# Two-layer hybrid block: the sums of squares in the gated delta rule as two fp32r matmuls of high and low parts

## What is computed

```
def l2_normalize(x):
    return xf * lax.rsqrt(jnp.sum(xf * xf, axis=-1, keepdims=True) + EPS)
...
qkv = jax.nn.silu(causal_short_conv(g_qkv, conv_w))
gq, gk, gv = split(qkv)                    # 8 heads of 128 each
gq = l2_normalize(gq) * 128 ** -0.5
gk = l2_normalize(gk)
o_gdn = gated_delta_rule_chunked(gq, gk, gv, g, beta)
o_gdn = rms_norm_2(o_gdn, gdn_norm_g) * silu(z)
```

## Time and profile before

| | |
|---|---|
| median of 3 runs | 1613.04 us |
| lowest and highest | 1610.92 and 1615.45 us |
| the profiled execution | 1611.96 us, its span 1609.8 us |
| mean granted TensorE clock of the span | 0.997 |
| delta rule in the span | from about 836 to 1239 us |

### The profile page before, as it was taken

One profiled execution on the slowest core, in us unless ns is written; L12 is line 12 of the kernel. 1 busy time (PEld: TensorE's weight loads), 2 busy tenths in 40 slices (PEclk: granted clock), 3 DMA queues, 4 the chain that ended last, 5 costly groups with the idle time before them and its releaser, 6 DMA issues.

```text
span 1609.8 us, 23976 instructions
## 1 busy us (share of the span) xinstructions
PE 1572.8 (98%) x9289; PEld 1258.7 (78%) x9289; DVE 1146.2 (71%) x1742; ACT 762.7 (47%) x1179; POOL 231.8 (14%) x206
## 2 busy tenths in 40 slices
PE   8999999999999999999999999999999999999999
PEld 5778778888888877667677878878787888888887
DVE  5867764867676787887767677585775477777768
ACT  6444444736363656325555345353443373626263
POOL 0544320000000002233200504005050000000000
PEclk9999999999999999999999999999999999999999
DMA  5222225323232412223113132131220351414131
GB/s 156 77 66 67 67 65 174 114 93 116 90 120 71 126 46 66 66 66 94 27 49 93 27 83 67 55 91 52 68 67 27 119 168 54 145 65 144 66 105 53
DMA packets 196816, 135.39 MB, mean 84 GB/s; under 512 B 9627, under 2 KB 184236, under 8 KB 196708
## 3 DMA queue, kind: packets, MB, share of 16 engines
q1 hardware_dynamic: 196708, 133.90, 27.8%
HBM read 131.70 MB, written 2.18 MB: 83 GB/s over the span
## 4 chain that ended last, share of the span: by engine, by line
PE 79%; DVE 11%; ACT 4%; issue 3%; DMA 1%; POOL 1%; SPq 0%; POOLq 0%; ACTq 0%; DVEq 0%; PEldq 0%
PE bank L244 10%; PE bank L246 10%; PE bank L245 10%; PE bank L1187 6%; PE bank L1189 6%; PE bank L1188 6%; PE bank L351 4%; PE bank L353 4%; PE bank L352 4%; PE bank L2193 4%; DVE arena L2500 3%; DVE w_lo L228 2%; ACT w_hi L224 2%; PE bank L2019 1%; PE bank L1748 1%
## 5 line engine op out<-in xcount | busy, mean ns | idle before, releaser
L228 DVE TENSOR_TENSOR w_lo<-raw,w_hi 128x1024 fp32r<-128x1024 f32 x152 | 191.5, 1260 | 73.0 <-ACT w_hi L224 71.8
L244 PE MATMUL bank<-m_hi,w_hi 128*128 128x512 f32 x584 | 231.8, 397 | 8.8 <-DVE w_lo L228 4.4
L245 PE MATMUL bank<-m_lo,w_hi 128*128 128x512 f32 x584 | 228.2, 391 | 0.0
L246 PE MATMUL bank<-m_hi,w_lo 128*128 128x512 f32 x584 | 228.2, 391 | 0.0
L224 ACT CAST w_hi<-raw 128x1024 fp32r<-128x1024 f32 x168 | 175.2, 1043 | 85.7 <-PE bank L246 48.9
L1219 ACT CAST d_hi<-arena 128x1024 fp32r<-128x1024 f32 x112 | 117.7, 1051 | 130.1 <-PE bank L1189 130.1
L1224 DVE TENSOR_TENSOR d_lo<-arena,d_hi 128x1024 fp32r<-128x1024 f32 x112 | 135.8, 1217 | 10.1 <-ACT d_hi L1219 10.0
L244 PEld LDWEIGHTS bank<-m_hi,w_hi 128*128 128x128 f32 x584 | 110.1, 188 | 38.5 <-DVE w_lo L228 10.8
L244 PE MATMUL bank<-h_hi,w_hi 128*128 128x512 f32 x344 | 135.4, 394 | 1.0 <-DVE w_lo L228 1.0
L246 PE MATMUL bank<-h_hi,w_lo 128*128 128x512 f32 x344 | 134.0, 390 | 0.0
L245 PE MATMUL bank<-h_lo,w_hi 128*128 128x512 f32 x344 | 134.0, 389 | 0.0
(11 more groups left out here) (352 smaller groups left out, 3333.2 us busy)
## 6 DMA issues: line engine op xcount, KB each, us to landing
raw<-in_w_in SPq DMA_DIRECT2D x64, 512.0 KB, 3.8
raw<-in_l_w_ff SPq DMA_DIRECT2D x32, 512.0 KB, 4.1
arena<-in_l_w_ff SPq DMA_DIRECT2D x32, 512.0 KB, 5.6
raw<-in_w_mlp_up SPq DMA_DIRECT2D x32, 512.0 KB, 4.0
arena<-in_w_mlp_down SPq DMA_DIRECT2D x32, 512.0 KB, 5.5
raw<-in_l_w_in SPq DMA_DIRECT2D x24, 512.0 KB, 3.8
raw<-in_l_w_out SPq DMA_DIRECT2D x8, 512.0 KB, 4.1
arena<-gb_rows SPq DMA_DIRECT2D x16, 256.0 KB, 4.7
```

The costliest lines, as they stand in the source:

```text
L228: dve.tensor_tensor(w_lo[q.par][:], raw[q.par][:], w_hi[q.par][:].bitcast(F32), ALU.subtract).then_inc(s["w_ready"], 1)
L244: pe.matmul(g_bank[q.par][:], w_hi[q.par][:, k], hi[:, k], start=(k == 0), stop=False)
L245: pe.matmul(g_bank[q.par][:], w_hi[q.par][:, k], lo[:, k], start=False, stop=False)
L246: last = pe.matmul(g_bank[q.par][:], w_lo[q.par][:, k], hi[:, k], start=False, stop=(k == KT - 1))
```

## The change

Both kinds of sums are made as two fp32r matmuls: the tile of squares is split into a high part (rounded by ScalarE) and a low part (subtracted by VectorE), each is multiplied by a matrix of ones in fp32r, and the two accumulate in one bank. For the keys the cast stands on ScalarE right behind the square, and the subtraction on VectorE at u = 2 and u = 4, between `silu` and `dve_split`. For the outputs the casts stand on ScalarE between `out_squares` and `out_roots`, and the subtractions on VectorE between `out_total` and `out_gate`; TensorE makes the sums after k = 5 instead of k = 3 of panel 0 (for the last pair the place stays). The new tiles lie in memory that is not in use at that time (`l_hi2` over `rr`, `l_lo2` in place of the key squares, `t_hi2` over `kb`, `t_lo2` in place of the output squares). So that the places fit, `ub` grows from 516 to 544 elements, which moves what follows it in the arena by 28 elements.

```diff
+        ones_r = sb("ones_r", [P, P], F32R)
...
-        ub = take(SEQ + CONV)
+        ub = take(SEQ + 32)
...
             def l2_sum(p, e):
-                pe.wait_ge(s["l_sq"], 2 * p + e + 1)
-                pe.matmul(b[2 * e][:], ones[:], sq2[:, e], start=True, stop=True).then_inc(s["l_ss"], 1)
+                pe.wait_ge(s["l_lo"], 2 * p + e + 1)
+                pe.matmul(b[2 * e][:], ones_r[:], l_hi2[:, e], start=True, stop=False)
+                pe.matmul(b[2 * e][:], ones_r[:], l_lo2[:, e], start=False, stop=True).then_inc(s["l_ss"], 1)
...
             def out_sums(p):
                 for e in range(2):
-                    pe.wait_ge(s["oo_t"], 2 * p + e + 1)
-                    pe.matmul(b[2 * e][:], ones[:], o_sq[:, e], start=True, stop=True).then_inc(s["oo_ss"], 1)
+                    pe.wait_ge(s["oo_tl"], 2 * p + e + 1)
+                    pe.matmul(b[2 * e][:], ones_r[:], t_hi2[:, e], start=True, stop=False)
+                    pe.matmul(b[2 * e][:], ones_r[:], t_lo2[:, e], start=False, stop=True).then_inc(s["oo_ss"], 1)
...
-                            if k == 3 and u == 0:
+                            if k == 5 and u == 0:
                                 out_sums(p - 1)
...
                 act.activation(sq2[:, e], qkv[:, 3 * e + 1], ACT.Square).then_inc(s["l_sq"], 1)
+                act.wait_ge(s["l_sq"], 2 * p + e + 1)
+                act.copy(l_hi2[:, e], sq2[:, e]).then_inc(s["l_hi"], 1)
...
+            def out_sum_high(p):
+                for e in range(2):
+                    act.wait_ge(s["oo_t"], 2 * p + e + 1)
+                    act.copy(t_hi2[:, e], o_sq[:, e]).then_inc(s["oo_th"], 1)
...
                     out_squares(p - 1)
+                    out_sum_high(p - 1)
                     out_roots(p - 1)
...
+            dve.tensor_copy(ones_r[:], ones[:]).then_inc(s["memsets"], 1)
             dve.sem_inc(s["ub0"], 1)
...
+            def out_sum_low(p, e):
+                dve.wait_ge(s["oo_th"], 2 * p + e + 1)
+                dve.tensor_tensor(t_lo2[:, e], o_sq[:, e], t_hi2[:, e].bitcast(F32), ALU.subtract).then_inc(s["oo_tl"], 1)
+
+            def l2_low(p, e):
+                dve.wait_ge(s["l_hi"], 2 * p + e + 1)
+                dve.tensor_tensor(l_lo2[:, e], sq2[:, e], l_hi2[:, e].bitcast(F32), ALU.subtract).then_inc(s["l_lo"], 1)
...
                     out_total(p - 1, 0)
                     out_total(p - 1, 1)
+                    out_sum_low(p - 1, 0)
+                    out_sum_low(p - 1, 1)
                     out_gate(p - 1)
...
                     if u:
                         silu(p, u - 1)
+                    if u in (2, 4):
+                        l2_low(p, u // 2 - 1)
                     dve_split(dve, gdn_panel(p, u + 2))
                     conv(p, u)
```

More of the change, by code:

```diff
@@ L149, in build @@
                 nc.sbuf_tensor("d_lo1", [P, 2, SEQ], F32R) as d_lo1:
+            pass
+        with nc.sbuf_tensor("sum_room0", [P, 2048], F32), nc.sbuf_tensor("l_hi2", [P, 2, SEQ], F32R) as l_hi2, \
+                nc.sbuf_tensor("l_lo2", [P, 2, SEQ], F32R) as l_lo2, nc.sbuf_tensor("sum_room1", [P, 7200], F32), \
+                nc.sbuf_tensor("t_hi2", [P, 2, SEQ], F32R) as t_hi2, nc.sbuf_tensor("t_lo2", [P, 2, SEQ], F32R) as t_lo2:
             pass
@@ L2131, in build @@
         gc_b, be_b = take(2, SEQ), take(2, SEQ)
+        assert at[0] == 2048
         rr, sq2 = take(2, SEQ), take(2, SEQ)
@@ L2138, in build @@
         dec = [take(TT, P) for _ in range(2)]
+        assert at[0] == 11296
         kb, ek = take(2, SEQ), take(2, SEQ)
@@ L2165, in build @@
              "dm_b dm_c dec_r ek_a ek_b ek_c kk_ps kk_r qk_ps qk_r kbe_r qd_r tok_ps tok_sb al_r yy_ps y_sb2 "
-             "z_ps t_r u_ps2 u_sb w_sb ws_ps vn_r kv_ps st2 oo_ps oo_sq oo_q oo_t oo_ss oo_ln oo_r oo_y2 oo_y3 oo_y4 oo_hi "
+             "z_ps t_r u_ps2 u_sb w_sb ws_ps vn_r kv_ps st2 oo_ps oo_sq oo_q oo_t oo_th oo_tl l_hi l_lo oo_ss oo_ln oo_r oo_y2 oo_y3 oo_y4 oo_hi "
              "gdn_done", reuse=True)
@@ L2477, in act_gdn @@
             out_squares(PAIRS - 1)
+            out_sum_high(PAIRS - 1)
             out_roots(PAIRS - 1)
@@ L2486, in dve_gdn @@
                 dve.memset(t_f[e][bot, :, 0:CHUNK], 0.0).then_inc(s["memsets"], 1)
-            dve.wait_ge(s["memsets"], 7)
+            dve.wait_ge(s["memsets"], 8)
             def conv(p, u):
@@ L2687, in dve_gdn @@
             out_total(p, 1)
+            out_sum_low(p, 0)
+            out_sum_low(p, 1)
             out_gate(p)
```

## The result

| | before | changed |
|---|---|---|
| median of 8 runs | 1612.93 us | 1617.82 us |
| lowest and highest | 1609.56 and 1615.45 | 1615.36 and 1620.37 |
| ratio of the runs | | 1.0033, 95% interval 1.0020 to 1.0046 |
| profiled execution, and its span | 1611.96, 1609.8 | 1619.75, 1617.9 |

The kernel became slower by 4.9 us by the medians and 5.3 by the ratio (0.0033 x 1613), with an interval of 3.2 to 7.4. It lies at the bound of what can be told from no change (0.3%, 4.8 us).

The account below looks back on a forecast made before the run. The ScalarE and VectorE loop was taken to set the pace up to panel 7, not PE. Loop and tail (+3.8 us) plus two clock falls (+2.9) gave +6.7 on 1613.04: 1619.7 us, range 1614.8 to 1623.8.

Parts of the forecast that it names:

- my own forecast: The loop's loss plus one to four clock falls: 1618.3 to 1622.6 us, given chance 0.52.
- rival 1: Panel 5 of each pair: stalls stay without a clock fall, only the loop counts; 1616.8 us, chance 0.30.
- The bound: Up to panel 7 in every pair, the ScalarE and VectorE loop sets the pace, though PE is 98% busy.
- rival 2: PE is the bound after all, decided at panel 7; its 6.5 us saving counts: 1606.5 us, chance 0.04.
- u = 4: VectorE's new subtraction ahead of panel 6's split delays the loop 0.61 us in each of four pairs: 2.4 us.
- The loop's start: Output sums two eighths later delay logarithms and `conv_in(0)`: 0.68 us in each of three pairs, 2.0 us.
- The stall: PE waits about 2.5 us mid panel 5 for head 1's low part, each pair; hidden with 0.13 to spare.
- Rival 3: Panel 5's stall is not hidden: 0.5 us more per pair; 1621.7 with two falls, 1624.6 with four; chance 0.12.
- rival 4: Ones in fp32r cost 0.86 per matmul, like fp32; PE works 6.5 us more: about 1626, chance 0.02.
- The tail: Last pair's output sums: PE and the roots come earlier despite a 0.13 wait, -0.65 us.
- Sum without the clock: Loop at u = 4, loop's start and tail: 4 x 0.61 + 3 x 0.68 - 0.65 = +3.8 us.
- The clock: After panel 5's stalls: two of four followed by a fall of PE's clock, 1.45 us each, +2.9 us.

Follow-up runs that it names:

- both half changes: The change for the key sums alone (1614.68 us against 1612.73) and for the output sums alone (1613.61 us), each with the other sums as before.
- keys only: Against the kernel before: key sums split as in the change, output sums left as one fp32 matmul each after k = 3; 1614.68 us against 1612.73, ratio 1.0016.
- the kernel without the stall, sum behind panel 6: The change with the key sum of head 1 moved on PE from the middle of panel 5 to behind panel 6; 1618.90 us, ratio 1.0041.
- the loop in a better order: VectorE's convolution ahead of the split: 1604.34 us with fp32 sums, 1602.04 with only output sums split; a mixed order with both sums split, 1596.84.
- outputs only: Against the kernel before: output sums split as in the change, after k = 5, key sums left as before; 1613.61 us, ratio 1.0002.
- low part at u = 5: The change with head 1's key sum behind panel 6 and its subtraction on VectorE moved from u = 4 to u = 5; 1613.48 us, ratio 1.0005.
- output sums after k = 3: The change with the output sums moved back from k = 5 to k = 3 of panel 0; 1614.47 us against 1613.44, ratio 1.0013.
- all three places: The change with head 1's low part at u = 5, its sum behind panel 6, and output sums after k = 3; 1611.15 us, ratio 0.9989.

## Why the prediction was right, and where its sizes were off

The measured 1617.8 lies in the range, but under the span that I gave my own forecast (one to four falls, 1618.3 to 1622.6) and nearer to rival 1 (1616.8).

- **The bound.** Right. Against 98% busy, the loop of ScalarE and VectorE sets the pace up to panel 8; rival 2 (PE is the bound) is out by both half changes. One reading was wrong: of the "4.9 us in 6 waits" for `w_lo` only four, 2.8 us, stood before panel 7; one stood in pair 0 (1.16) and one behind the last pair (0.97).
- **u = 4.** Forecast 0.61 a pair, measured 0.60.
- **The loop's start.** Forecast 0.68, measured 0.68. Cast, subtraction and sums took the times of the rows; PE did not wait at the sums.
- **The stall.** Forecast 2.5 and hidden with 0.13 to spare. Measured 2.3, and hidden: PE came 0.13 to 0.15 before the bank in pairs 0, 2 and 3 and 0.33 in pair 1, and taking the stall away shortened no stage. Rival 3 did not happen. Nor did rival 4, whose sum was wrong: two matmuls of 0.86 in place of one are 16 x 0.86 = 13.8 us more of PE, not 6.5.
- **The tail.** Forecast -0.65, measured -0.68.
- **Sum without the clock.** Forecast +3.8. From the stages 4 x 0.60 + 3 x 0.68 - 0.68 = 3.8; the two profiled executions differ by 5.9 over the delta rule, of which 1.6 is one more fall of the clock at the start of a scan and some 0.5 are single steps that one pair of one execution has and its neighbours don't.
- **The clock.** Here the size was off, and so was its ground. I took "two of the four stalls" to be followed by a fall at 1.45 us each, +2.9. The profiles with this stall show 3 falls in 12 at 1.2 each: 4 x 3/12 x 1.2 = 1.2 us, and all three lie in one execution. In the profile of the changed kernel itself there was none, which is rival 1's picture, and PEclk was 1 in panels 5 and 6, against what I had said it would show. That a stall of PE can lower the clock was right: 3 in 12, 4 in 4 and 4 in 4 for 2.3, 3.4 and 6.4 us, none in 36 without a stall. That 1.6 us is too short and 2.76 long enough was not: see the last section. With 1.2 in place of 2.9 the sum is +5.0, beside the 4.9 and 5.3 measured. Forecast 1619.7, measured 1617.8.

That +5.0 and 4.9 meet so well is in part luck. By the granted clock of all the runs, the change lost about 1.4 us more to the clock than the kernel before (0.9958 against 0.9967), but which falls made that up is not on record: keys only, with the same stalls, lost no more than before (0.9965 against 0.9967), and the kernel without the stall lost more (0.9952). So the timed worth of the stall in the change stays open.

The advice of the Trainium skill that I had set against the trace ("TensorE: Matmul & The Clock Gate", "Why this matters for your kernels") lets stalls of 2.3 us pass. In 9 of 12 the runs agree and in 3 they don't, so it is no bound under which one is safe.

## What to carry to other kernels

An engine that is busy for 98% of the span may still have slack at one place of each round, and that place decides: follow the chain to the wait that recurs, and price a change by what it adds there. The same subtraction cost 0.6 us behind a late step and nothing one step further on, and the same sums moved two eighths later cost 0.7 where their operands had long been ready. A saving on a hidden engine need not be lost: with the loop in a better order most of the outputs' part came through, and by the account of PE's waits most of the keys' part too.

## What the runs showed that I had not expected

The clock of TensorE falls at other places too, in some executions and not in others, at a like price. About 12 us before the output squares of a pair, where the 64x64 tiles of `inverse` end and the 128x128 tiles of `scan` begin, PE waits no longer than 0.6 us, and still the clock falls there now and then: pair 3 before, pairs 1 and 3 with the change, none in several others, 10 pairs of 56 in all profiles. The windows of the changed kernel, pair 1 with a fall and pair 2 without:

```profile
1023.00:1028.00 5.00, 4.62 (x32) 4.46 (x31) 1.52 (x3) 2.29 (x5) 0.00 (x0) 0.77 0.00 0
...
1123.00:1128.00 5.00, 4.62 (x41) 4.46 (x40) 2.00 (x4) 2.59 (x5) 0.00 (x0) 1.00 0.01 5
```

Pair 1's rest is 51.4 and pair 2's 49.8, 1.6 us for a fall.

Nor does the length of a wait alone decide. Three waits of PE stand ahead of the delta rule in all 14 profiles, alike in each: 1.46 us at about 210 was followed by a fall in 3 of 14, 1.56 us at about 598 in 6 of 14, and the 2.76 us of the earlier trace rows in 11 of 14. The 1.56 us brought the clock down more often than the 2.3 us in panel 5 did. It is the wait of the earlier trace rows, behind which the kernel before kept its clock in its profile; here it is in the profile of the change:

```profile
598.06 0.50 PE L1645 MATMUL bank<-h_hi,w_hi 128*128 128x512 f32 x1 [1.56 <-DVE h_lo L1438]
...
599.03 0.63 PE L1645 MATMUL bank<-h_hi,w_hi 128*128 128x512 f32 x1
599.46 0.63 PE L1646 MATMUL bank<-h_lo,w_hi 128*128 128x512 f32 x1
```

The last two are 0.43 apart, 1.2 GHz. One trace that shows a fall, or none, behind one wait says little about the next execution; the prediction had one.

The granted clock accounts for nearly all of the scatter between executions of one kernel. Each of the 70 runs of the kernel before has its mean granted clock on record, from 0.993 to 0.999, and its time follows it: 1.5 us more for each 0.001 less (correlation -0.96). Taking that out leaves 0.55 of the 2.0 us of standard deviation. It also allows an estimate of each difference at equal clock, by means and against the runs of before that were made beside it (for the change, against all 70):

| kernel | mean clock, and before's | difference | at equal clock | by the stages |
|---|---|---|---|---|
| the change | 0.9958, 0.9967 | +5.4 | +4.0 | +3.8 |
| keys only | 0.9965, 0.9967 | +2.0 | +1.8 | +2.4 |
| outputs only | 0.9972, 0.9967 | +0.8 | +1.5 | +1.4 |
| sum behind panel 6 | 0.9952, 0.9967 | +6.5 | +4.2 | +3.8 |
| low part at u = 5 | 0.9972, 0.9967 | +1.2 | +1.9 | +1.4 |
| output sums after k = 3 | 0.9948, 0.9965 | +1.6 | -0.9 | -0.4 |
| all three places | 0.9957, 0.9965 | -1.6 | -2.7 | -2.8 |

The stages that I read from single profiles agree with the runs within 0.6 us once the clock is taken out.
